# A two-block forward pass on one core: a small triangular substitution moved ahead, block transfers on two queues, and other tile addresses

## The reference

```
k_beta = kc * bc[..., None]
diff = gc[..., :, None] - gc[..., None, :]
decay = exp(where(tril, diff, -inf))
m = where(strict, einsum('bhncd,bhnsd->bhncs', k_beta, kc) * decay, 0.0)
lmat = m + eye(CHUNK)
sol = triangular_solve(lmat, rhs, lower=True, unit_diagonal=True)
u, w = sol[..., :dv], sol[..., dv:]
a_qk = einsum('bhncd,bhnsd->bhncs', qc, kc) * decay
```

## Time and profile before

| | us |
|---|---|
| median of 3 runs | 911.99 |
| lowest, highest | 910.93, 915.26 |
| the profiled execution, whole | 914.05 |
| its span from first to last instruction | 911.1 |
| TensorE busy in the span | 894.8 |
| VectorE busy | 555.2 |
| ScalarE busy | 291.6 |
| DMA, mean over the span | 170 GB/s |

### The profile page before, as it was taken

The page is one execution under the profiler, slowest core; times in us unless marked ns, Lnnn a source line. Parts: engine busy times, 40 slices in busy tenths (PEclk is TensorE's granted clock), DMA queues, the critical chain, the costliest instruction groups (busy, mean ns, idle before and its releaser), DMA issues.

```text
span 911.1 us, 13462 instructions
## 1 busy us (share of the span) xinstructions
PE 894.8 (98%) x4595; PEld 718.6 (79%) x4595; DVE 555.2 (61%) x972; ACT 291.6 (32%) x594; POOL 72.4 (8%) x138
## 2 busy tenths in 40 slices
PE   9999998999999999999999999999999999999998
PEld 7887776687888888888888888888888777567877
DVE  7248467346877777776653344397787463875554
ACT  6234456523322222222210111253221113454710
POOL 0000000000110001000010000000000000000000
PEclk9999999999999999999999999999999999999999
DMA  8766543253766555566555655568555232221553
GB/s 273 243 193 190 160 139 116 89 158 128 234 198 198 195 184 188 196 200 198 185 185 192 193 195 198 169 217 256 185 151 168 87 94 93 93 82 59 182 190 137
DMA packets 53861, 154.73 MB, mean 170 GB/s; under 512 B 9628, under 2 KB 15020, under 8 KB 53688
## 3 DMA queue, kind: packets, MB, share of 16 engines
q1 hardware_dynamic: 22320, 75.70, 26.3%
q0 software_dynamic: 19008, 69.21, 23.3%
q10 hardware_dynamic: 12488, 9.19, 3.3%
HBM read 149.60 MB, written 4.49 MB: 169 GB/s over the span
## 4 chain that ended last, share of the span: by engine, by line
PE 87%; DVE 5%; issue 3%; ACT 2%; DMA 2%; DVEq 0%; SPq 0%; POOLq 0%; ACTq 0%
PE bank L672 75%; DMA HI<-wstream 1%; PE bank L731 1%; DVE LO L1643 1%; PE bank L1113 1%; PE bank L809 1%; PE bank L1093 1%; PE bank L833 1%; PE bank L823 1%; DMA RAW<-wstream 1%; PE bank L1104 1%; PE bank L1024 0%; DVE SQ L1625 0%; PE bank L1046 0%; ACT GH L1234 0%
## 5 line engine op out<-in xcount | busy, mean ns | idle before, releaser
L672 PE MATMUL bank<-GH,HI 128*128 128x512 f32 (+1 forms) x724 | 293.0, 405 | 1.5 <-issue 1.5
L672 PE MATMUL bank<-GH,LO 128*128 128x512 f32 (+1 forms) x724 | 281.9, 389 | 0.0
L672 PE MATMUL bank<-GL,HI 128*128 128x512 f32 (+1 forms) x724 | 281.3, 389 | 0.0
L1643 DVE TENSOR_TENSOR LO<-RAW,HI 128x1024 fp32r<-128x1024 f32 x88 | 107.5, 1222 | 118.2 <-DMA HI<-wstream 117.2
L672 PEld LDWEIGHTS bank<-GH,HI 128*128 128x128 f32 x724 | 136.0, 188 | 36.8 <-issue 10.1
L672 PEld LDWEIGHTS bank<-GH,LO 128*128 128x128 f32 x724 | 135.9, 188 | 28.9
L672 PEld LDWEIGHTS bank<-GL,HI 128*128 128x128 f32 x724 | 136.3, 188 | 23.5
L654 POOL DMA_DIRECT2D HI<-wstream x132 | 69.8, 529 | 814.0 <-PE bank L672 804.1
L1355 ACT ACTIVATE YC<-AB,PAR 128x512 f32<-128x512 f32 x44 | 36.0, 818 | 140.6 <-DVE AB L1807 140.6
L672 PE MATMUL bank<-AH,HI 128*128 128x512 f32 x176 | 69.3, 394 | 0.0
L672 PE MATMUL bank<-AH,LO 128*128 128x512 f32 x176 | 69.0, 392 | 0.0
(11 more groups left out here) (310 smaller groups left out, 1159.0 us busy)
## 6 DMA issues: line engine op xcount, KB each, us to landing
RAW<-wstream SPq DMA_DIRECT2D x135, 512.0 KB, 3.7
HI<-wstream POOLq DMA_DIRECT2D x132, 512.0 KB, 4.9
X<-x_t SPq DMA_DIRECT2D x8, 256.0 KB, 7.5
NCB<-out_t ACTq DMA_DIRECT2D x8, 256.0 KB, 4.0
out_t<-X ACTq DMA_DIRECT2D x8, 256.0 KB, 5.6
XR<-out_t ACTq DMA_DIRECT2D x8, 256.0 KB, 3.6
out_t<-XR SPq DMA_DIRECT2D x7, 256.0 KB, 3.4
EG<-out_t ACTq DMA_DIRECT2D x1, 1024.0 KB, 4.6
```

The lines of the kernel that those rows point to most:

```text
L672: mm = pe.matmul(out, a, b, start=(first and n == 0), stop=(last and n == 2))
L1643: dve.tensor_tensor(LO[:, u % RING, :], RAW[:, u % RING, :], HI[:, u % RING, :].bitcast(F32), ALU.subtract).then_inc(unit_split, 1)
```

## The change

1. Order. `solve` moves from behind `dfv` 7 to behind `dfv` 6; `AQ` 2, `T2` 0, `AQ` 3 move from ahead of `dfv` 7 to behind it, together with `scatter` 0. `scatter` 1 moves from behind query part (1, 1) to ahead of part (1, 0).
2. Queues. Of the eight blocks of NT and of the eight of XI, ScalarE's queue keeps the first four. SyncE's does the other four: those of NT right behind its load of unit 113, those of XI right behind its load of unit 117. SyncE's loop of loads is cut in two for that, with units 112 to 119 written out.
3. Addresses. The first tile starts at 16640, and PAR goes to the end of the arena, which then begins at a multiple of 512. X, GH, GL, RAW and HI stay at multiples of 128.

```diff
-               [("AQ", 2), ("T2", 0), ("AQ", 3)], [("solve", 0), ("scatter", 0)]]
+               [("solve", 0)], [("AQ", 2), ("T2", 0), ("AQ", 3), ("scatter", 0)]]
...
-    + QUERIES_KEYS[:8] + [("T2", 1)] + QUERIES_KEYS[8:10] + [("scatter", 1)] + QUERIES_KEYS[10:21] + [("X", (0, 3)), ("X", (1, 3))] + QUERIES_KEYS[21:24]
+    + QUERIES_KEYS[:8] + [("T2", 1), ("scatter", 1)] + QUERIES_KEYS[8:21] + [("X", (0, 3)), ("X", (1, 3))] + QUERIES_KEYS[21:24]
...
-        here = [16512]
+        here = [16640]
...
-        PAR = place("PAR", [P, NPAR], F32)
...
+        assert arena % 512 == 0, arena
+        PAR = place("PAR", [P, NPAR], F32, arena + 118 * KB)
...
+            for u in range(U_DFQK, U_DFQK + 8):
+                load(u // 4, u % 4)
+                if u == U_DFQK + 1:
+                    sp.wait_ge(nt_made, NB)
+                    for q in range(4, P // SUB):
+                        r = slice(SUB * q, SUB * (q + 1))
+                        sp.dma_start(sub_blocks(896, q), NT[r, :, :, r].rearrange("p h b t -> p (h b) t"))\
+                          .then_inc(scratch_stored, 16)
+                elif u == U_DFQK + 5:
+                    sp.wait_ge(scratch_stored, STORED_XS)
+                    sp.wait_ge(zero_made, 2)
+                    for q in range(4, P // SUB):
+                        r = slice(SUB * q, SUB * (q + 1))
+                        sp.dma_start(XI[r, :, :, r].rearrange("p h b t -> p (h b) t"), sub_blocks(960, q))\
+                          .then_inc(scratch_landed, 16)
...
-                    for q in range(P // SUB):
+                    for q in range(4):
...
-                    for q in range(P // SUB):
+                    for q in range(4):
```

More of the change, by code:

```diff
@@ L388, in build @@
         KB = 1024
+        assert arena % 512 == 0, arena
+        PAR = place("PAR", [P, NPAR], F32, arena + 118 * KB)
+        assert arena + 118 * KB + 4 * NPAR <= 229368, arena
         MT = place("MT", [P, 8, T], F32, arena)
@@ L631, in _, with load @@
             load_x(7)
-            with sp.Fori(1, UNITS // 4) as i:
-                for s in range(RING):
[L635 to L638, removed]
+            def load(i, s):
+                sp.wait_ge(unit_done, 4 * i + (s - RING + 1))
+                sp.dma_start(RAW[:, s, :],
+                             wstream[bass.ds(2 * i + s // 2, 1), :, 1024 * (s % 2):1024 * (s % 2 + 1)]
+                             .rearrange("o p n -> p (o n)")).then_inc(w_landed[s], 16)
+            with sp.Fori(1, U_DFQK // 4) as i:
+                for s in range(RING):
+                    load(i, s)
+            for u in range(U_DFQK, U_DFQK + 8):
[13 more added lines that the diff above has]
+                          .then_inc(scratch_landed, 16)
+            with sp.Fori(U_DFQK // 4 + 2, UNITS // 4) as i:
+                for s in range(RING):
+                    load(i, s)
             for m in range(KC - 1):
```

## The result

The changed kernel takes 915.26 us (median of 20 runs, 912.96 to 920.23) against 912.13 (20 runs, 910.93 to 915.26): a ratio of 1.0037, interval 1.0027 to 1.0048. The profiled execution took 914.92 us with a span of 913.0, against 914.05 and 911.1. So it lies within 0.5%, as forecast, and inside the range, but 3.1 us above the kernel before, where the sum had +0.9. From about line 650 on, a line of the changed kernel stands 22 further down than in the kernel before (L1954 for L1932).

A forecast was written before the change was run, and what follows sets the result against it. TensorE, busy 119.86 of 120 us in the changed stretch, was taken as the bound; +2.9 (T2 1 wait) - 1.6 - 0.4 (addresses) = +0.9 us took the median from 911.99 to 912.9 us, range 909 to 917.

The forecast's parts named there:

- the sum: Whole kernel: +2.9 (T2 1), -1.6 (720 matmuls), -0.4 (small ones) = +0.9 us; known ends -3.2 and +4.2.
- T2 1 waits: TensorE after query unit 0: T2 1 waits 2.9 us for VectorE's AQ 3 product; ends 1.34 and 4.16 us.
- Body: The substitution on VectorE once MS has landed, 684.83 to 693.18 in the kernel before: 8.35 us.
- tail: On VectorE behind the substitution: low part of unit 114 (1.14 us) and four operations (2.48 us), together 3.62 us.
- MS is issued at about 675.05, 1.3 us earlier: ScalarE, with four blocks on SyncE, issues MS once VectorE finishes the key scalars, at about 675.05: 1.3 us earlier.
- Addresses: TensorE matmuls with operands in the arena get 2.25 ns faster once it is aligned: 1.6 us plus 0.4 us gained.
- The part for the 720 matmuls: 528 matmuls with AH or AL and 192 with MH or ML, 2.25 ns less each: 1.6 us gained.
- the 0.4 for the small ones: About 1300 small matmuls, most with an arena operand: 0.4 us gained, between 0 and 2.9 us.
- addresses worth nothing: Rival: the new addresses make no matmul faster, only the T2 1 wait counts: 914.9 us; chance 0.17.
- nothing beyond the 1.3 us counted: NT blocks on SyncE delay no load; splitting over two queues saves 1.3 us of issue and no transfer time.
- The late scatter: Rival: SyncE's XI blocks land at 707.1 for 704.21; TensorE waits 2.9 us more at first Y: 917.8 us; chance 0.10.
- The short wait: Rival: MS goes out 0.3 us ahead of the ring's loads, T2 1 waits about 1.35 us: 909 to 911.4; chance 0.19.

The follow-up runs named there:

- the second timing: The changed kernel, unaltered, timed again on another chip beside the kernel before: 916.89 us, ratio 1.0046.
- the two fillers: Twelve repeated matmuls added ahead of T2 1's wait, in the changed kernel (914.45 us) and in the changed kernel with the old addresses (915.55 us).
- the four timings with the wait unfilled: Changed kernel, twice: 915.26 and 916.89 us; changed kernel with old addresses: 917.75 us; changed kernel with all eight blocks on ScalarE's queue: 917.95 us.
- The filled kernel: The changed kernel with 12 matmuls of query unit 1 done once more ahead of T2 1's wait: 914.45 us, ratio 1.0024.

## Why the prediction came out as it did

**T2 1 waits: right, a little short.** Forecast 2.9 us, measured 3.44, within its ends of 1.34 and 4.16. Body (8.36 for 8.35) and tail (3.54 to the end of AQ 3's product and 0.14 to the start on TensorE, for 3.62) were as read. The step that failed in it is "MS is issued at about 675.05, 1.3 us earlier". In the clock of the kernel before, MS went out at 673.93 + 2.12 = 676.05, 0.3 us earlier than the earlier trace rows. I had taken the key scalars as the last thing ahead of it; they were done (ScalarE used them at 672.98), and MS waited for the landing of the NT blocks, 3.94 us, a step missing from the sum. A faster landing of MS, 5.7 for 6.3, gave half of the lost 1.0 us back.

**Addresses: the size nearly right, the reason wrong.** TensorE's 2.12 us in the trace at 688, and 1.1 to 1.9 us in the times of the three kernels that differ from the kernel before in addresses alone and go at 226.7 ns (medians, and means at full clock), stand against 2.0. The part for the 720 matmuls, 1.6 us, is what their start-to-start times give; the 0.4 for the small ones stays unproven. The rival "addresses worth nothing" is refuted. The Trainium skill, "SBUF — State Buffer", section "Specifications (TRN2)", gives cachelines of 16 bytes; I had set it against the term. Moving every tile by 32 or 64 bytes does cost nothing, which agrees with it, but it says nothing of two tiles read together, and that is where the 2.2 ns are. The Trainium skill, "TensorE: Matmul & The Clock Gate", section "Step-by-step: what each phase is for", calls the read ports for data and for weights independent. The rows differ from that by 1%: 228.9 against 226.7 ns, by the distance of the two tiles alone. Where in the chip this arises no run shows.

**Queues.** Worth 0.7 to 1.0 us on MS in the new order, forecast 1.3; nothing in the old one. The step "nothing beyond the 1.3 us counted" took the issue time as saved whole, where the blocks' slower landing took back 1.4 of 2.2 us. The late scatter did not happen, nor did anything else behind load 117.

**The short wait.** Refuted by 3.44 us. Its premise failed: MS didn't go out 0.3 us ahead of the ring's load but 0.8 behind it (SyncE issued the load of unit 114 at 673.17, MS went at 673.93). MS took 4.2 us to land in one kernel (T2 1 moved) and 5.3 to 6.0 in the other kernels, so a shorter wait was possible.

**What the sum lacked: the clock.** At full clock the changed kernel is at 914.21 and the kernel before at 912.15 to 912.38, a difference of 1.8 to 2.1, which is what 3.4 us of wait less 1.1 to 1.9 of addresses gives. The other 1.1 us of the median, 2.7 in the second timing, come with executions in which the clock fell, 20 of 26 against 34 of 88. That idling at T2 1 is the cause is shown by the two fillers: same start of T2 1 at best, more work, and still less time, with 13 of 17 executions at full clock against 6 of 38 in the four timings with the wait unfilled. The 2.4 us were gained on one chip; the 2.2 compare two. The filled kernel's nine executions at full clock average 914.19, the changed kernel's six 914.21 on another chip, as they should if the filler moves nothing but the clock. The prediction counted an idle microsecond as a microsecond. The Trainium skill, "TensorE: Matmul & The Clock Gate", section "What's actually happening", says that TensorE's clock is halved after it has been idle, and that the number of matmuls at the lower clock at a kernel's start differs between runs of one kernel. The rows agree for a pause inside a kernel: 0.50 behind waits of 3.2 to 4.2 us in three of four profiled executions, and not in the fourth. Used on the prediction's own wait, with eight matmuls at 0.2 us each, it would have made a rival at 912.9 + 1.6 = 914.5.

Long waits are not the only ones with a fall behind them. The profile with the arena alone moved, which has the old order and no wait at T2 1, shows one early in the kernel (TensorE's timeline, then one-us windows):

```profile
153.54 0.33 PE L811 MATMUL bank<-KH,MH 64*128 64x128 f32 x2 [1.52 <-DVE KL L1744]
...
154.00:155.00 1.00, 1.00 (x18) 0.85 (x16) 0.97 (x3) 0.93 (x2) 0.00 (x0) 1.00 0.02 8
155.00:156.00 1.00, 1.00 (x8) 0.96 (x6) 1.00 (x2) 0.00 (x0) 0.00 (x0) 0.60 0.00 0
...
161.00:162.00 1.00, 1.00 (x6) 0.47 (x4) 0.03 (x1) 0.94 (x3) 0.00 (x0) 0.50 0.00 0
162.00:163.00 1.00, 1.00 (x10) 0.59 (x8) 0.67 (x1) 0.50 (x2) 0.00 (x0) 0.99 0.00 0
```

The kernel before has this wait of 1.5 us too (at 153.84), without the fall in its profile. So this is one place where its 34 executions below full clock can have lost it. These average 913.4 us, the 54 at full clock 912.2.

**Luck.** The sum for the profiled execution, 914.9, came out at 914.92, but not by its terms: the span was 913.0 for 912.0, and the time outside the span 1.9 us for 2.95. The median stayed inside the range although a price, that of the clock, was missing, since the range was made wide for other reasons.

**Open.** Moving T2 1 gives 912.29 us where the old order gives 910.9; the difference lies in executions with a fallen clock, whose place no profile of it shows. Later in the kernel the changed one loses 1.0 us more, half of which it has back by the end. In its profile TensorE waits at 870.87 for a QT, released late behind a low part that waited for HI to land, which it did not before (VectorE, then TensorE):

```profile
868.84 1.23 DVE L1665 TENSOR_TENSOR LO<-RAW,HI 128x1024 fp32r<-128x1024 f32 x1 [1.24 <-DMA HI<-wstream]
...
870.87 0.63 PE L1145 MATMUL bank<-CON,QT 128*128 128x128 f32 x4 [0.92 <-DVE QT L2204]
```

The second profile of the changed kernel waits in the same stretch, at 868.25 and 870.06, and behind these shorter waits too the clock stands at 0.50 for about 3.4 us, from 870.3 on:

```profile
868.25 1.26 PE L1145 MATMUL bank<-CON,QT 128*128 128x128 f32 x8 [1.25 <-DVE QT L2199]
870.06 0.62 PE L694 MATMUL bank<-FH,HI 128*128 128x512 f32 x1 [0.55 <-DVE ZT L1657]
```

That these waits follow from the shift of 1.4 us, by which the later transfers start, was not tested.

## What to carry to other kernels

Moving a step ahead is free only if nothing that the critical engine needs stands behind it: here four operations were put behind a wait for a load, and TensorE, which had not paused in this stretch, paused. For such a wait, list everything before the load as well, the landing of the stores that it reads back included. If stores or loads are split over two queues to save issue time, look at when they land as well. Give a pause of a few microseconds on TensorE a second price, that of a fallen clock behind it, to be paid in part of the executions; repeated matmuls in the pause won back more than they cost here, though not having the pause is better still (910.9 us). And place matmul data and weights at the same offset within 128 bytes, or within 256, which is all that the fast placements here show, before looking at absolute alignment.

## What the runs showed of the hardware

- A 128x512 fp32r matmul stream goes at 226.7 ns per matmul where data and weight tile start at the same place within 128 bytes (0/0, 32/32, 64/64; the same within 256 bytes in all of them) and at 228.8 to 229.0 ns where they are 64 apart (64/0, 0/64). That is 1.0% of such streams.
- The clock fell to 1.2 GHz for 3.4 to 6.8 us behind idle stretches of 3.2 to 4.2 us, with 0.426 us between matmuls in place of 0.227, and not in every execution: a wait of 3.3 us once went without it.
- It also fell behind shorter waits: for about 6.8 us behind one of 1.52 us (at 153.54, arena alone moved), and for about 3.4 us behind two of 1.25 and 0.55 us (at 868.25, the changed kernel again). Behind one of 2.04 us (the filled kernel) it did not.
- From the issue of ScalarE's last 16 KB store of the gather to the issue of MS, which waited for the stores to land, it was 2.5 us with all eight on one queue (one profile) and 3.9 to 5.1 us with four on each of two queues (five profiles whose chains show it).
